# A two-model stack on one core: scan tables from transposed powers, the scan's input gathered inside the feed-forward block, and another order of scaling and squaring in two projections

## What is computed

```python
def first_block(x, ...):
    for i in range(DEPTH):                       # mixer kinds 0, 1, 2, 0
        h = rms_norm(x, norm_mix_g[i])
        ...
        x = x + mix
        h = rms_norm(x, norm_ffn_g[i])
        x = x + swiglu(h, ffn_w_gate_up[i], ffn_w_down[i])

def fourier_mixer(h, w_out):
    f = jnp.fft.fft2(hg, axes=(1, 3), norm="ortho").real
    return f.reshape(b, s, d) @ w_out

def _s5_direction(u, lam_re, lam_im, log_dt, b_re, b_im, c_re, c_im, reverse):
    lam_bar = jnp.exp(lam * dt)
    b_bar = ((lam_bar - 1.0) / lam)[..., None] * lax.complex(b_re, b_im)
    bu = ...                                     # u times b_bar, per group of 16 features, 64 states
    _, hs = lax.associative_scan(combine, (a, bu), axis=1, reverse=reverse)
    return jnp.einsum('gpn,bsgn->bsgp', c, hs).real

def s5_mixer(h, ...):
    y = (y_fwd + y_bwd).reshape(b, s, d) + d_skip * hf
    g = jax.nn.gelu(y)
    val, gate = jnp.split(g @ w_glu, 2, axis=-1)
    return val * jax.nn.sigmoid(gate)
```

## Time and profile before

| | us | |
|---|---|---|
| median of 3 runs | 2930.91 | 2927.89 to 2933.01 |
| the profiled execution | 2930.03 | its span 2928.2, mean granted TensorE clock 0.973 |
| PE busy | 2796.3 | 95% of the span |
| DVE busy | 1570.8 | 54% |
| ACT busy | 1134.6 | 39% |
| POOL busy | 339.3 | 12% |

### The profile page before, as it was taken

The page is one execution under the profiler, slowest core; times in us unless marked ns, Lnnn a source line. Parts: engine busy times, 40 slices in busy tenths (PEclk is TensorE's granted clock), DMA queues, the critical chain, the costliest instruction groups (busy, mean ns, idle before and its releaser), DMA issues. The chain is left out here.

```text
span 2928.2 us, 38710 instructions
## 1 busy us (share of the span) xinstructions
PE 2796.3 (95%) x15552; PEld 2277.3 (78%) x15552; DVE 1570.8 (54%) x2341; ACT 1134.6 (39%) x1792; POOL 339.3 (12%) x426
## 2 busy tenths in 40 slices
PE   9999999599999999999999899999999999999887
PEld 8788888488888877777788578888988888776665
DVE  7776664754434434554535654344654344664656
ACT  5332232364222324645647342223432123543443
POOL 0333221710000001111112300000000000110100
PEclk9999999799999999999999799999999999999989
DMA  4245557554444223222222323222222222211101
GB/s 142 96 147 170 156 155 222 192 160 120 130 127 116 96 75 110 70 92 80 87 94 91 126 101 101 101 88 103 69 101 89 99 100 101 82 49 40 57 15 46
DMA packets 116020, 307.08 MB, mean 105 GB/s; under 512 B 28176, under 2 KB 73808, under 8 KB 87296
## 3 DMA queue, kind: packets, MB, share of 16 engines
q1 hardware_dynamic: 108064, 278.39, 29.0%
q10 hardware_dynamic: 6336, 21.76, 2.1%
q0 software_dynamic: 1440, 4.46, 0.5%
HBM read 266.91 MB, written 41.85 MB: 105 GB/s over the span
## 5 line engine op out<-in xcount | busy, mean ns | idle before, releaser
L94 PE MATMUL ps<-hh_,wh_ 128*128 128x512 f32 x2184 | 867.2, 397 | 8.8 <-DVE hl_ L135 5.1
L94 PE MATMUL ps<-hh_,wl_ 128*128 128x512 f32 x2184 | 853.9, 391 | 0.0
L94 PE MATMUL ps<-hl_,wh_ 128*128 128x512 f32 x2184 | 853.7, 391 | 0.0
L121 DVE TENSOR_TENSOR wl_<-raw_,wh_ 128x2048 fp32r<-128x2048 f32 (+4 forms) x245 | 483.2, 1975 | 503.6 <-ACT wh_ L117 503.1
L117 ACT ACTIVATE wh_<-raw_ 128x2048 fp32r<-128x2048 f32 (+3 forms) x244 | 400.6, 1648 | 351.6 <-PE ps L94 331.2
L94 PEld LDWEIGHTS ps<-hh_,wh_ 128*128 128x128 f32 x2184 | 412.2, 189 | 107.0 <-issue 9.3
L94 PEld LDWEIGHTS ps<-hh_,wl_ 128*128 128x128 f32 x2184 | 411.9, 189 | 87.4
L94 PEld LDWEIGHTS ps<-hl_,wh_ 128*128 128x128 f32 x2184 | 412.4, 189 | 86.2 <-issue 2.9
L94 PE MATMUL ps<-ah_,wh_ 128*128 128x512 f32 x704 | 275.1, 391 | 0.0
L94 PE MATMUL ps<-al_,wh_ 128*128 128x512 f32 x704 | 274.0, 389 | 0.0
L94 PE MATMUL ps<-ah_,wl_ 128*128 128x512 f32 x704 | 274.0, 389 | 0.0
(11 more groups left out here) (363 smaller groups left out, 3584.5 us busy)
## 6 DMA issues: line engine op xcount, KB each, us to landing
raw_<-in_w SPq DMA_DIRECT2D x203, 1024.0 KB, 5.0
sO<-s5ce_ SPq DMA_DIRECT2D x32, 256.0 KB, 3.7
sW<-s5wt_ SPq DMA_DIRECT2D x16, 512.0 KB, 6.0
sA<-os_ SPq DMA_DIRECT2D x24, 256.0 KB, 2.1
ol_<-sA SPq DMA_DIRECT2D x24, 256.0 KB, 3.6
sT<-sK SPq DMA_DIRECT2D x32, 128.0 KB, 4.0
wh_<-sO ACTq DMA_DIRECT2D x4, 1024.0 KB, 6.1
wl_<-sO ACTq DMA_DIRECT2D x4, 1024.0 KB, 7.5
```

The costliest lines, as they stand in the source:

```text
L94: return self.e.matmul(out, lhsT, rhs, start=start, stop=stop, skip_group_check=True)
L121: return Nothing() if self.e is None else self.e.tensor_tensor(out, a, b, op)
```

## The change

1. **Tables.** The powers `G` are transposed once (eight TensorE transposes, two ScalarE copies into `P.flat`) and stored in `sG`. For each chunk SyncE loads them back in eight transfers of 64 KB, spread over the partitions (`chunk_sync`, `p.gx`), and loads B already transposed and repeated by the host (`s5bt` into `bx`, 512 KB). VectorE's sums write the state table straight to `wt`. The eight transposes and two copies per chunk are gone. For the small products GpSimd makes `wn` by six operations on 128x64 (`scaled_b`), which are recorded ahead of its multiplies for the state table. A chunk takes nine slots in place of eight and the first begins four slots later.
2. **U.** `U` lies on the memory of `hl`, and the runs 0 and 1 of `spread` are issued in feed-forward 0's second half, at m = 3 and m = 6.
3. **Row sums.** VectorE adds the square of m = 6 too, and `rows_tensor` has two groups.
4. **Projections.** ScalarE makes the scaled copy ahead of the square; VectorE adds the square of m - 1 ahead of `hl` of m, and that of m = 7 last. In the Fourier projection the splits of weights are also placed differently between the background calls (on ScalarE as in the part shown of VectorE).
5. **Gated output projection.** In its first loop the second pair runs two row blocks behind the first.

The diff, cut to its core:

```diff
@@ square_vector
-    if 0 < m < (6 if s in LAST else 8):
+    if 0 < m < (7 if s == 2 else 6 if s in LAST else 8):
@@ project_scalar
-    square_scalar(K, ac, s, m, "x", s, m)
-    if g is not None:
-        if old:
-            ac.wait_ge(*K.at(*old))
-        gained_scalar(K, ac, s, g, m)
+    ac.wait_ge(*K.at("x", s, m))
+    if old:
+        ac.wait_ge(*K.at(*old))
+    gained_scalar(K, ac, s, g, m)
+    square_scalar(K, ac, s, m, "x", s, m)
@@ project_vector
     dv.mark("out", *p)
-    square_vector(K, dv, s, m)
-    if g is not None:
-        gained_vector(K, dv, s, g, m)
+    square_vector(K, dv, s, m - 1)
+    gained_vector(K, dv, s, g, m)
+    if m == 7:
+        square_vector(K, dv, s, m)
@@ ffn_sync
+            if f == 0 and half and m == 3:
+                spread(K, sp, 0, "U", range(8))
+            if f == 0 and half and m == 6:
+                spread(K, sp, 1, "U", range(8))
@@ fourier_vector
+    lows(K, dv, 8)
     for m in range(8):
-        lows(K, dv, 4)
-        dv.bg()
-        lows(K, dv, 4)
         project_vector(K, dv, s + 1, m, nxt, ("pj", s + 1, m))
...
+        dv.bg()
+        if m < 7:
+            lows(K, dv, 8)
         dv.bg()
@@ prep_sync
+    for _ in range(PREP_FIRST + 2):
+        yield
+    sp.wait_ge(*K.at("p.gt", 1))
+    sp.dma(d["sG"].rearrange("r b q n -> q (r b) n"), P.flat.rearrange("p (b n) -> p b n", b=8)).then_inc(*K.lane("s5sG").up("p.sG"))
+    yield
+    sp.wait_ge(*K.at("p.w"))
+    sp.dma(P.bx[:, :, :], d["s5bt"][0]).then_inc(*K.lane("s5gx").up())
+    sp.wait_ge(*K.at("p.sG"))
+    chunk_sync(K, sp, 0, range(8))
...
+        sp.wait_ge(*K.at("p.f", pc, 1))
+        sp.dma(d["sW"][un][:, 1024 * hf:1024 * hf + 1024], P.flat).then_inc(*K.lane("s5sW").up("p.sW", pc))
         if pc < 15:
-            sp.wait_ge(*K.at("p.f", pc, 1))
+            sp.wait_ge(*K.at("p.wn", pc))
             sp.dma(P.bc[:, :, :, :], d["s5bc"][pc + 1]).then_inc(*K.lane("s5bc").up("p.bc", pc + 1))
-        yield
-        yield
+            sp.dma(P.bx[:, :, :], d["s5bt"][pc + 1]).then_inc(*K.lane("s5gx").up())
+        yield
+        if pc < 15:
+            chunk_sync(K, sp, pc + 1, range(4))
+        yield
+        if pc < 15:
+            chunk_sync(K, sp, pc + 1, range(4, 8))
         yield
...
+def chunk_sync(K, sp, pc, powers):
+
+    for i in powers:
+        sp.dma(K.prep.G[16 * i:16 * i + 16, :, :, :].rearrange("p r s g -> p r (s g)"),
+               bass.AP(K.d["sG"].tensor, 512 * pc + 8192 * i, [[0, 16], [65536, 2], [1, 512]])).then_inc(
+            *K.lane("s5gx").up(*(("p.gx", pc) if i == 7 else ())))
@@ prep_scalar
-        for r in range(2):
-            ac.wait_ge(*K.at("p.t", pc, r))
-            ac.act(P.wt[:, :, r, :], K.mb["p.t", pc, r].rearrange("p (g x) -> p g x", g=4), ACT.Copy).then_inc(*ac.up("p.wt", pc, r))
-            ac.mark("out", "p.t", pc, r)
@@ prep_vector
-            out = (P.ce, P.wn)[x]
+            out = P.ce[:, 0, :, :, :], P.wt[:, :, 0, :]
             n, v, er, ei, xr, xi = prep_views(P, pc, x)
-            dv.wait_ge(*K.at("p.bc", pc))
+            dv.wait_ge(*K.at(("p.bc", "p.gx")[x], pc))
...
+            if x:
+                dv.wait_ge(*(K.at("p.sW", pc - 1) if pc else K.at("p.sG")))
...
-                dv.tt(out[:, 1, :, :, :], v[0], v[1], ALU.add).then_inc(*dv.up("p.f", pc, x))
+                dv.tt(P.wt[:, :, 1, :], v[0], v[1], ALU.add).then_inc(*dv.up("p.f", pc, x))
@@ prep_views
+def scaled_b(K, po, pc):
+
+    P = K.prep
+    t = [P.t2[:, 512 + 64 * i:576 + 64 * i].rearrange("p (g x) -> p g x", g=4) for i in range(2)]
+    fr, fi = (P.fb[:, r, 4 * pc:4 * pc + 4].rearrange("p (g x) -> p g x", x=1).broadcast_to([128, 4, 16]) for r in range(2))
+    br, bi = P.bc[:, 0, :, :], P.bc[:, 1, :, :]
+    po.wait_ge(*K.at("p.fb"))
+    for r, (x, y, op) in enumerate(((br, bi, ALU.subtract), (bi, br, ALU.add))):
+        po.tt(t[0], x, fr, ALU.mult).then_inc(*po.up())
+        po.tt(t[1], y, fi, ALU.mult).then_inc(*po.up())
...
+        po.tt(P.wn[:, r, :, :], t[0], t[1], op).then_inc(*po.up(*(("p.wn", pc) if r else ())))
@@ prep_gpsimd
             if x:
                 po.wait_ge(*K.at("p.f", pc, 0))
+                scaled_b(K, po, pc)
@@ prep_tensor
+    for r in range(2):
...
+        for i in range(4):
+            m = pe.tr(b[:, 128 * i:128 * i + 128], P.gx[:, r, 128 * i:128 * i + 128], K.ident)
+        m.then_inc(*pe.up("p.gp", r))
...
-        pe.wait_ge(*K.at("p.f", pc, 1))
+        pe.wait_ge(*K.at("p.wn", pc))
...
-        for r in range(2):
-            b = K.mb.take("p.t", pc, r)
-            pe.wait_ge(*K.after(pe, K.mb, "p.t", pc, r))
-            for g in range(4):
-                m = pe.tr(b[:, 128 * g:128 * g + 128], wn[:, r, g, :, :].rearrange("p s x -> p (s x)"), K.ident)
-            m.then_inc(*pe.up("p.t", pc, r))
@@ rows_tensor
-    for n, (event, squares) in enumerate(((("ss", 2, 5), K.ssq), (("sqr", 2, 6), K.sq[0]), (("sqr", 2, 7), K.sq[1]))):
+    for n, (event, squares) in enumerate(((("ss", 2, 6), K.ssq), (("sqr", 2, 7), K.sq[1]))):
@@ spread
-    e.wait_ge(*K.at("p.t", 15, 1))
-    e.wait_ge(*K.at("p.sO", 15, 1))
+    e.wait_ge(*K.at("u", 0, 1, NH - 1))
@@ the GLU's first pair, on TensorE
-    for k in range(8):
-        pe.wait_ge(*K.at("s.gl", k))
+    for at in range(10):
+        if at < 8:
+            pe.wait_ge(*K.at("s.gl", at))
         for m in range(2):
+            k = at - 2 * m
+            if not 0 <= k < 8:
+                continue
@@ memory
+    with ExitStack() as under:
+        K.U = K.sb(under, "U", [128, 64, 64])
     K.hl = sb("hl", [128, 8, 512], R32)
@@ sync
     prep_end(K, sp)
-    for n in range(2):
-        spread(K, sp, n, "U", range(8))
     staged_sync(K, sp, 7)
     spread(K, sp, 2, "U", range(8))
```

113 lines of the change are left out of this document (64 added, 49 removed).

## The result

The changed kernel takes 2973.73 us (median of 4 runs, 2968.39 to 2976.33) where the kernel before takes 2930.97 (4 runs): a ratio of 1.0150, 95% interval 1.0134 to 1.0167. It is 42.8 us slower. The forecast was 2937.5, with a range from 2925 to 2948.

A forecast was written before the change was run, and what follows sets the result against it. TensorE was taken to bound the first feed-forward block, then one serial chain up to the first product on U. Gains of 19.4 us against a cost of 26.5 gave net +7.1: 2937.5 us, range 2925 to 2948.

The forecast's parts named there:

- the chain of the seam: From T to the first product on U: 10.85 us before, forecast 28.4 longer, 26.5 net of a warmer clock.
- T: Start of the last addition to x in the first feed-forward block: 489.59 us before, forecast 471.
- 16 chunks give 13.9 ... They hide nothing else, since TensorE is full.: First feed-forward block: taking each chunk's eight transposes off TensorE saves 0.87 us a chunk, 13.9 us in all.
- Rival 2: First feed-forward block: late reload or GpSimd operations make product groups wait, 8 us together, 2945.5 us; chance 0.13.
- Two chunks fall off the end.: Chunks 14 and 15 run behind the last x: 1.3 us gained, first product on U at T + 39.2, 26.5 net cost.
- The gather of U, taken early, thus gives little by itself.: End of the first feed-forward block: the early gather ends before the row sums, so gives little by itself.
- rival 1: Block's end: SyncE not held up, gathers under 0.75 us, reload and B land earlier: net +2.3, 2932.8 us; chance 0.28.
- Row sums at the low clock.: Behind chunk 15: two groups of 16 records after TensorE's idling take 5.9 us, bounds 4.1 to 6.5.
- The first 64 records after it now find a warm clock.: First products on U: 64 records take 7.5 us in place of 9.30, so 1.9 us comes back.
- The projections.: Fourier projection: TensorE's waits for h fall from 4.5 to 1.8 us; with the clock 4.0 saved, ends 2.5 and 5.3.
- "0.6" for the mix and "0.5" for the gate: Mix: its 0.59 us wait goes, 0.6 saved; gate products: second pair two steps later, 0.5 saved, ends -1 and 2.
- if TensorE idles between 130 and 465: First feed-forward block: a sign that would show the forecast wrong, TensorE being expected to stay full there.

The follow-up runs named there:

- b_last: The changed kernel with each chunk's small products two slots later and GpSimd's scaled B behind its two state-table multiplies: 2952.23 us, ratio 1.0065 against the kernel before.
- old_tail2: The kernel before with every chunk 18 background slots later, so chunks 14 and 15 come behind the last x, with old tables: 2952.00 us, ratio 1.0083.
- old_rest: The kernel before with its own tables and parts 2 to 5 of the change: 2928.02 us, ratio 0.9996 against the kernel before.
- gather_late: The changed kernel with gathers of U runs 0 and 1 issued behind all table work again: 2963.69 us, ratio 1.0116 against the kernel before.
- old_best: The kernel before with parts 2 to 5, gather run 1 at m = 5 and the first chunk's small products one slot later: 2928.47 us, ratio 0.9992.

## Why the prediction was wrong, step by step

The sign was right, the chain of the seam was the right one, and the size was off by 35.7 us: the sum gave +7.1, and +42.8 was measured. In the terms of the sum, T came 22.5 us late, the chain behind it was 12.3 longer than forecast, and the first products on U lost 2.5 more; that is 37.3 in the profiles. That the medians differ by 35.7 has two reasons: the stretches behind, where the profile of before was long, and profiled executions that are not the median ones. The step that failed first is that new work on VectorE and GpSimd was put at nothing because TensorE was full; the second is the time at which SyncE was to be free at the end of the block.

- **"16 chunks give 13.9 ... They hide nothing else, since TensorE is full."** This failed most. TensorE was full because VectorE kept up with some time to spare. The change added 35.3 us to VectorE's waits for GpSimd (53.9 against 18.6 for the chunks' tables, from 130 to 470 us, two lines of each list above), two and a half times what the transposes were to give TensorE. Some 26 of these came out of VectorE's waits for ScalarE (14.7 and 11.1 less), the other 9 or 10 did not. The bound that I had set, "nothing if hidden, and up to 4", came from a comparison of 2.5 us a chunk with 7 us of mean idle time. But idle time counts in an engine that works in order only where it lies ahead of the instruction that someone waits for. Measured: T was to be at 471.3 and was at 493.85. Of these 22.5 us, 16.5 are the waits for the scaled B and al; the rest is, by the windows, the lower clock behind them and small delays, which I did not separate. b_last shows that the order on GpSimd alone decides some 19 us, 6.9 of them in T and 8.3 in the seam. No run takes away the reload alone, which raised the DMA share of this stretch from 0.50 to 0.63.
- **Rival 2, "TensorE stalls in the full stretch"**, named the mechanism and priced it at "1 to 3 us at a few places, 8 together". It was 16.5 us of waits in seven places, and T 22.5 late; with a chance of 0.13 it had been put too low. Of its two places, chunk 13 was right (4.3 us) and chunk 0 had no wait; its argument against itself, that elsewhere the products come eight slots behind the load, did not help at the other places, where the wait was for the chain of VectorE and GpSimd and not for a load. The sum was built as if forecast and rival excluded each other; both happened.
- **"Two chunks fall off the end."** Right, and shown by itself (old_tail2: 24.7 us). The chain of T + 39.2 came to T + 51.5. The steps: I took B and C of chunk 14 as landed, and they came at T + 8.2; from there the output table was ready at T + 14.1 in place of 5.6, the powers at T + 16.5 in place of 9.5, chunk 14 at T + 24.1 in place of 16.4, B for chunk 15 at T + 28.5 in place of 19.9, chunk 15 at T + 42.1 in place of 31.4, and the row sums took 7.1 in place of 5.9. About 7 us are the powers: the second gathers were to begin at T - 5.3 and began at T + 1.5, since the forecast had left out the loads for chunk 14 that stand ahead of them on SyncE (B and C, whose issue took 5.27 us, and the transposed B, 1.95). The other 5 are small errors of one sign. The six operations took 2.8 us for a forecast of 2.4.
- **"The gather of U, taken early, thus gives little by itself."** Right for the seam, and too kind: undoing it saved 10 us, since the gathers made others late. Eight gathers took 7.46 us of SyncE the first time and 9.03 the second. That is near the 9.9 taken from the earlier trace rows, and rival 1, which needed a gather of under 0.75 us, is out: 1.13 us a gather. The price of 2.1 us for a small load did not hold here: the load of B and C took 14.6.
- **Row sums at the low clock.** Right in kind: clock 0.50 from 536 to 544 us, 3.68 and 3.60 us for 16 records each. The 7.1 us of both lie over the 5.9 taken and over its bound of 6.5: the group at 582.93, by which it was priced, ran at a clock of 0.68 (582.9 to 588.4 us of before), not at 0.50.
- **"The first 64 records after it now find a warm clock."** This failed: 9.92 us where 7.5 was taken, and 9.30 before. The clock was 0.50 until 550 us. The row sums, 7.1 us of work behind 40 us with 2.2 in them, did not bring it back. So the 1.9 us that the sum took off did not come, and 0.6 was added.
- **The projections.** "The waits fall to 1.8": 1.2 in one piece, at a clock of 1.00 in place of 0.54. The forecast of 4.0 compares with 4.6 in old_rest at the products of chunk 0, the wait there taken out, and 3.05 at the chunk's transposes, behind the low clock (both from single profiles, good to some 3 us); that kernel also shows that the gain is lost at chunk 0 unless the chunk's products move too.
- **"0.6" for the mix and "0.5" for the gate.** Nothing can be seen of either. From the first product on U to feed-forward 1 the two profiles stay 44.9 to 45.0 us apart, with the gate's products between; over the attention mixer and the mix the changed kernel comes 4.9 closer and old_tail2, with the old order, 4.6. TensorE waited 1.5 us for hl in the gate's part after, in place of 2.1 for a weight split before.

What the signs named as wrong did show up: "if TensorE idles between 130 and 465" it did, for 12.2 us, and GpSimd waited in chunk 14 for B and C, not for the reload alone.

## What to carry to other kernels

An engine's mean idle share is no cover for work given to its neighbour: list what the in-order engine waits for in each period, and see on which side of that value the new work stands (six small GpSimd operations cost some 19 us more ahead of a product than behind it). When background work is laid out in fixed slots beside foreground work, count first how many periods fit, and then at which place of the foreground each step now meets it. A transfer that is moved early moves others late: at a seam with busy DMA engines, look at who waits for the load or store that now stands behind it.

## What was not expected of the hardware

- A 128 KB load that lands in 2.1 us on quiet queues took 14.6 from issue to landing beside 1 MB loads on another queue, and its issue alone blocked SyncE for 5.27 us (13.5 and 5.44 in gather_late).
- The landing of a 256 KB store beside two 1 MB loads took some 10 us (474.82 to 484.54 in old_best), long enough that issuing its reader ahead of the next row block's store, and not behind it, had no effect.
